# One fp32 transformer program on a single NeuronCore: norms and rotations moved beside dense tiles, token parts handled one by one

## What is computed

```python
def first_block(x, c, ...):            # 512 tokens
    h = _rms(x, norm1_w) * (1 + sc1) + sh1
    x = x + g1 * _hybrid_mixer(h, ...)     # SSD scan, dilated attention, pooling, gated and summed
    h = _rms(x, norm2_w) * (1 + sc2) + sh2
    x = x + g2 * (jnp.square(jax.nn.relu(h @ w_ff1)) @ w_ff2)
# in the mixer, for the scan's output y, in 2 groups of 512 columns:
    y = y * silu(z); y = y * lax.rsqrt(mean(y*y) + EPS); y_ssd = (y * ssd_norm_w) @ w_ssd_out
def second_block(x, c, ctx, c_ctx, ...):   # 4 layers over 512 latent + 256 context tokens
    for i in range(4):                 # mixers: window attention, latent attention, mLSTM, window attention
        h_l = rmsnorm(x_lat, g_pre) * (1.0 + sc_l) + sh_l
        h_c = rmsnorm(x_ctx, g_pre) * (1.0 + sc_c) + sh_c
        y_l, y_c = mixer(h_l, h_c, need_ctx=i < 3)
        x_lat = x_lat + gt_l * rmsnorm(y_l, g_post)
        if i < 3: x_ctx = x_ctx + gt_c * rmsnorm(y_c, g_post)
# latent attention (layer 1): q = rmsnorm(q_a) @ w_uq ; k, v = rmsnorm(kv_a) @ w_ukv ;
#   64 rotary columns of each query head and one shared rotary key are turned (RoPE)
# mLSTM (layer 2): two directions of decayed attention, summed, times sigmoid(o), rmsnorm by head, times silu(z)
```

## Time and profile before

| | us |
|---|---|
| median of 3 runs (lowest, highest) | 3195.63 (3194.22, 3197.38) |
| profiled execution: its own time | 3197.4 |
| profiled execution: span | 3195.6 |
| PE busy in the span | 2837.3 (89%) |
| DVE, ACT, POOL busy | 1682.6, 1216.8, 744.9 |
| mean granted TensorE clock | 0.947 of full |

### The profile page before, as it was taken

One profiled execution on the slowest core, in us unless ns is written; L12 is line 12 of the kernel. 1 busy time (PEld: TensorE's weight loads), 2 busy tenths in 40 slices (PEclk: granted clock), 3 DMA queues, 4 the chain that ended last, 5 costly groups with the idle time before them and its releaser, 6 DMA issues.

```text
span 3195.6 us, 39586 instructions
## 1 busy us (share of the span) xinstructions
PE 2837.3 (89%) x16088; PEld 2304.7 (72%) x16088; DVE 1682.6 (53%) x3080; ACT 1216.8 (38%) x2119; POOL 744.9 (23%) x160
## 2 busy tenths in 40 slices
PE   4976989989899999989898897899899988879896
PEld 2844877768686788769686675677589987658685
DVE  5875295162724999930387511254680246460483
ACT  3334224543123222242286333443442336342482
POOL 2410434304342444412100121100123210114101
PEclk7988999999899999999999998999999999899998
DMA  6402462202324555421101121101211331112101
GB/s 255 168 27 85 185 237 106 106 1 82 116 95 156 184 185 197 158 92 63 43 2 41 53 80 39 40 1 53 79 54 67 140 125 40 66 66 85 47 2 66
DMA packets 49621, 294.80 MB, mean 92 GB/s; under 512 B 4448, under 2 KB 5792, under 8 KB 19616
## 3 DMA queue, kind: packets, MB, share of 16 engines
q1 hardware_dynamic: 22464, 163.59, 14.2%
q10 hardware_dynamic: 26976, 128.68, 10.6%
HBM read 271.25 MB, written 21.00 MB: 91 GB/s over the span
## 4 chain that ended last, share of the span: by engine, by line
PE 61%; DVE 19%; ACT 4%; issue 3%; DMA 0%; ACTq 0%; DVEq 0%
PE psum L414 15%; PE psum L415 15%; PE psum L416 15%; DVE ada_temp L725 5%; PE psum L1636 2%; PE psum L873 2%; PE psum L1478 2%; PE psum L2783 2%; PE psum L1501 1%; PE psum L1657 1%; DVE pair_row L1686 1%; PE psum L1646 1%; DVE a_lo L882 1%; PE psum L1482 1%; DVE h L896 1%
## 5 line engine op out<-in xcount | busy, mean ns | idle before, releaser
L401 POOL TENSOR_TENSOR w_lo<-raw,w_hi 128x2048 fp32r<-128x2048 f32 x156 | 744.7, 4774 | 2408.7 <-ACT w_hi L409 2408.7
L414 PE MATMUL psum<-a_hi,w_hi 128*128 128x512 f32 (+3 forms) x1880 | 710.1, 378 | 105.5 <-DVE a_lo L882 66.5
L415 PE MATMUL psum<-a_lo,w_hi 128*128 128x512 f32 (+3 forms) x1880 | 699.3, 372 | 0.0
L416 PE MATMUL psum<-a_hi,w_lo 128*128 128x512 f32 (+3 forms) x1880 | 698.0, 371 | 0.0
L414 PEld LDWEIGHTS psum<-a_hi,w_hi 128*128 128x128 f32 (+1 forms) x1880 | 357.0, 190 | 193.8 <-issue 72.7
L725 DVE SCALAR_TENSOR_TENSOR ada_temp<-ada_ring,ada_rows 128x1024 f32<-128x1024 f32 x240 | 425.6, 1829 | 88.3 <-ACT ada_rows L685 54.6
L416 PEld LDWEIGHTS psum<-a_hi,w_lo 128*128 128x128 f32 (+1 forms) x1880 | 357.0, 190 | 63.1 <-issue 2.0
L415 PEld LDWEIGHTS psum<-a_lo,w_hi 128*128 128x128 f32 (+1 forms) x1880 | 357.6, 190 | 61.3 <-issue 3.2
L409 ACT ACTIVATE w_hi<-raw 128x2048 fp32r<-128x2048 f32 x156 | 298.0, 1911 | 246.6 <-DMA raw<-stream 98.2
L414 PE MATMUL psum<-w_hi,a_hi 128*128 128x256 f32 x800 | 229.6, 287 | 0.5 <-ACT c_gate_rows L2655 0.5
L415 PE MATMUL psum<-w_lo,a_hi 128*128 128x256 f32 x800 | 226.3, 283 | 0.0
(11 more groups left out here) (379 smaller groups left out, 4649.3 us busy)
## 6 DMA issues: line engine op xcount, KB each, us to landing
raw<-stream SPq DMA_DIRECT2D x156, 1024.0 KB, 4.8
ada_ring<-ada ACTq DMA_DIRECT2D x72, 1024.0 KB, 5.3
xres<-x_in ACTq DMA_DIRECT2D x4, 3072.0 KB, 9.5
x_in<-xres ACTq DMA_DIRECT2D x3, 3072.0 KB, 11.4
gates<-gate_part ACTq DMA_DIRECT2D x8, 768.0 KB, 4.4
c_rows_m<-rows_m ACTq DMA_DIRECT2D x2, 1536.0 KB, 7.9
c_og<-gates ACTq DMA_DIRECT2D x4, 768.0 KB, 4.2
c_z<-gates ACTq DMA_DIRECT2D x4, 768.0 KB, 6.4
```

The costliest lines, as they stand in the source:

```text
L401: pool.tensor_tensor(k.w_lo[:, r], k.raw[:, r], k.w_hi[:, r].bitcast(F32), ALU.subtract) \
L414: pe.matmul(out, lhs[0], rhs[0], start=start, stop=False)
L415: pe.matmul(out, lhs[0], rhs[1], start=False, stop=False)
L416: return pe.matmul(out, lhs[1], rhs[0], start=False, stop=stop)
```

## The change

1. `feature_major` puts out the LAT tiles of a pair of chunks, then their CTX tiles (before: LAT, CTX, LAT, CTX). `tile_place(t, n_parts)` gives chunk and part of tile t; all users of these tiles follow it. `pre_norm` says that CTX is waited for at tile 2, no more at tile 1.
2. `dense` gets `lead`: with `lead=2` the first two tiles are worked through together, product by product. Used in the first dense stage of all four layers (A0q, Bin, Cqk, A3q) and in ff1_0. In layer 3, whose q stage has no CTX tiles, the wait for CTX moves to the stage A3k.
3. `ssd_out`: both barriers go; DVE starts a group when its root is there, and PE goes on into the gates, waiting for chunk f of `y` only at the tile that reads it.
4. `layer_out` with two parts: `EarlySum` sums and roots LAT beside the last CTX tiles (behind tile 14 of the 16 tiles, 0 to 15); CTX's sum and root follow behind the barrier, and DVE starts on LAT as soon as the barrier is over. Its dense stage has 7 banks.
5. `mla_layer`: `LatentSteps` does norms, splits and the key's swap as a side of Bz, `QueryTurns` the query rotations as a side of Bk. The barriers behind Bz and Bq, and those of the steps, go; the one behind Bk stays. Bz, Bq and Bk have 6 banks.
6. Layer 2: no barrier between Cz and the attention. ACT loads head 0's gate at once, makes the decays of units 0 to 2, and only then waits for the stores. ACT's `scale` goes; DVE does that multiplication.

```diff
 def dense(... side=None, lead=1):
+                together = lead if lead > 1 and (i, s) == (0, 0) else 0
+                if together:
+                    pe.wait_ge(free.sem, free.at(together - ring))
+                    for j in range(len(slot_tiles[0][1])):
+                        if rhs_ready and (j, 0) in rhs_ready:
+                            pe.wait_ge(*rhs_ready[j, 0])
+                        for n, (cut, pairs) in enumerate(slot_tiles[:together]):
+                            last = products(pe, cut(bank(n)), *pairs[j], j == 0, j == len(pairs) - 1)
...
-    k.rhs_ready = split_at
+    k.rhs_ready = {(c, 2 * n): split_at[c, n] for c, n in split_at}
...
 def ssd_out(k, block, a, acc):
...
-    k.end_stage(block)
...
-    k.end_stage(block)
-    gated(k, block, a, y, [...], acc, B0, ada=...)
+    gated(k, block, a, y, [...], acc, B0 + 94208, rhs_ready=y_ready, ada=...)
...
+class EarlySum:
+    def on_tensor(self, pe, t):
+        if t == self.at:
+            pe.wait_ge(k.tile_free.sem, self.added)
+            pe.matmul(k.psum[:, 7, 0:t1 - t0], k.cst("ones"), self.total[:, t0:t1], ...)
+    def on_scalar(self, act, t):
+        if t == self.at:
+            act.wait_ge(self.summed.sem, self.summed.at(1))
+            root_rows(self.k, act, self.rstd, [self.part], D, (7,))
...
+class LatentSteps:
+    def on_scalar(self, act, t):
+        if t < 3:
+            act.activation(self.squares[:, t], self.raw[:, t, :], ACT.Square).then_inc(self.squared.sem, 1)
+        if t in (3, 5):
+            r = t // 2 - 1
+            act.wait_ge(self.summed.sem, self.summed.at(r + 1))
+            root_rows(k, act, self.rstd[:, r], [LAT, CTX], (256, 128)[r], (6, 7))
+    def on_tensor(self, pe, t):
+        if t in (1, 2, 4):
+            c = min(t - 1, 2)
+            pe.wait_ge(self.squared.sem, self.squared.at(c + 1))
+            if c == 2:
+                pe.wait_ge(self.rooted.sem, self.rooted.at(1))
+            for n, (t0, t1) in enumerate((LAT, CTX)):
+                last = pe.matmul(k.psum[:, 6 + n, 0:t1 - t0], k.cst("ones"), self.squares[:, c, t0:t1], ...)
+        if t == 7:
+            pe.wait_ge(self.rooted.sem, self.rooted.at(2))
+            pe.matmul(k.psum[:, 6, :], k.cst("swap"), self.raw[:, 3, 0:S], start=True, stop=True)
...
+class QueryTurns:
+    def on_tensor(self, pe, t):
+        n, rest = divmod(t, 5)
+        if rest == 0 and n < len(self.chunks):
+            if n >= 2:
+                pe.wait_ge(self.done.sem, self.done.at(n - 1))
+            pe.matmul(self.k.psum[:, 6 + n % 2, :], self.k.cst("swap"), self.chunks[n], start=True, stop=True)
...
 def decayed_attention(...):
-            dve.reciprocal(st[:, r, 2:4], st[:, r, 0:2]).then_inc(inverse.sem, 1)
-            dve.wait_ge(scaled.sem, scaled.at(n + 1))
-            dve.scalar_tensor_tensor(hsum[:, r], acc(n, 1)[:, 0:256], st[:, r, 3:4], forward[:, r], ALU.mult,
-                                     ALU.add).then_inc(taken.sem, 1)
+            ch(dve, dve.reciprocal(st[:, r, 2:4], st[:, r, 0:2]))
+            ch(dve, dve.tensor_scalar(hsum[:, r], acc(n, 0)[:, 0:256], st[:, r, 2:3], None, ALU.mult))
+            dve.scalar_tensor_tensor(hsum[:, r], acc(n, 1)[:, 0:256], st[:, r, 3:4], hsum[:, r], ALU.mult, ALU.add) \
```

More of the change, by code:

```diff
@@ L2160, in add_square @@
     def add_square(dve, i, t, ps):
-        t0, t1 = parts[t % n_parts]
+        t0, t1 = part(t)
         sq = square[:, t % 2, 0:t1 - t0]
@@ L2355, in mla_layer @@
           act_tile=lambda act, i, t, ps: (into(q, ACT.Copy, 0, -B_SCALE) if t < 16
-                                          else into(qr, ACT.Copy, -8, -B_SCALE))(act, i, t, ps))
+                                          else into(qr, ACT.Copy, -8, -B_SCALE))(act, i, t, ps),
+          barrier=False, n_banks=6)
     kv = [x[:, 2:3, :] for x in low]
@@ L2376, in take, with _ @@
         return act.activation(v[:, b, 512 * c:512 * c + 512], ps, ACT.Copy)
-    dense(k, block, ["Bk"], kv_tiles, act_tile=take)
-    rotate(k, block, [qr[:, c, 0:S] for c in range(4)], R0 + 73728)
+    @block.scalar
+    def _(act):
+        act.wait_ge(steps.normed.sem, key_turned)
+    turns = QueryTurns(k, [qr[:, c, 0:S] for c in range(4)], R0 + 92160)
+    dense(k, block, ["Bk"], kv_tiles, act_tile=take, n_banks=6, side=turns)
+    turns.over()
     b2 = (k.at("b2_hi", R0 + 24576, [P, KC, T2], F32R), k.at("b2_lo", A0, [P, KC, T2], F32R))
@@ L2631, in span @@
     def span(t):
-        n = S if t % 2 == 0 else SC
-        return n, (S if t % 2 else 0)
+        part = tile_place(t, 2)[1]
+        return (SC if part else S), (S if part else 0)
     def place(c):
         return 2 * (c % 4) + c // 4
-    dense(k, block, ["Cqk"], feature_major(a, KC, both), barrier=False,
+    dense(k, block, ["Cqk"], feature_major(a, KC, both), barrier=False, lead=2,
           act_tile=lambda act, i, t, ps: act.activation(pad[:, t % 8, 2:2 + span(t)[0]], ps[:, 0:span(t)[0]],
@@ L2847, in _ @@
                 decays(n + 1)
-            if 1 <= n <= N:
-                scale(n - 1)
+            if n == 1:
+                for place in range(3):
+                    act.wait_ge(saved[place].sem, 16 * len(range(place, 8, 3)))
+                load_z(0)
+                load_gate(1)
+                load_z(1)
             if n >= 2:
```

249 lines of the change are left out of this document (170 added, 79 removed).

## The result

The changed kernel takes **3101.9 us** (median of 4 runs, 3101.0 to 3107.4) beside 3196.5 us for the kernel before on the same chip: a ratio of 0.9707, with 0.9690 to 0.9723 as its interval. The forecast was 3097, in a range of 3085 to 3119. In another set, on another chip, the same program took 3102.6 us and the ratio was 0.9692 (0.9678 to 0.9706), so the ratio itself moves by some 0.15% from set to set.

A forecast was written before the change was run, and what follows sets the result against it. PE, busy 89% of the span, bounds the kernel; time is won in its pauses. Terms 18.3 + 21.2 + 12.0 + 25.0 + 9.0 + 7.5 + 7.0 = 100.0 us off 3197.4 give 3097.4, taken as 3097; range 3085 to 3119.

The forecast's parts named there:

- Two of my own signs of being wrong: PE waiting for ACT's root in Bz or for `y` in `gated`; a stage that the change leaves alone growing.
- `ssd_out`: Between norms' sums and gates: PE goes on without its 18.37 us stop; 18.3 us saved, lower bound 15.
- one rival: Moved DVE work beside dense tiles is held by POOL's splits, making the kernel slower: 3204 us, chance 0.01.
- Layer starts: First tile pairs of four layers: second LAT tile fits into the first's waits; 21.2 us with ff1_0, bounds 14 and 24.
- for ff1_0 [...] I estimate 0.5 of a possible 2: First feed-forward stage: two tiles together gain little because the start runs at half clock; 0.5 us saved.
- Layer ends: Three layer ends: LAT's early sum and root let DVE start 4.0 us earlier each; 12.0 us, bounds 6 and 13.
- 16.08 us follow to the next norm's first chunk, set by DVE's queue, and stay: Layer ends: the time from DVE's start to the next norm's first chunk stays 16.08 us.
- Behind Bz, Bq and Bk: Layer 1: pauses behind these stages go; 25.0 us behind Bz (bounds 20, 26), 9.0 behind Bq and Bk (4, 11).
- The rotations' 9.0: Query rotations moved into Bk: 6.6 us of pause and 2.4 of half clock at the attention's start saved.
- Side work in PE's way: Waits of `EarlySum`, `LatentSteps` and `QueryTurns` stop the dense tiles behind them: 3115 us, chance 0.10.
- The Trainium skill's 2.66 us for a table switch: Roots take 7.7 us, PE waits in Bz and at layer ends, the sum is 13 us smaller: 3110 us, chance 0.03.
- Layer 2: Pause before the attention shrinks, 7.5 us (bounds 4, 9.5); its units' stops at heads' roots shrink, 7.0 us (2, 10).

The follow-up runs named there:

- The idle matmuls: Changed kernel plus matmuls nobody reads in PE's pauses at layer starts and ends (3, 2 and 4), first feed-forward product one tile at a time: 3092.0 us.
- the doubled roots: Changed kernel with each of LatentSteps' two roots in stage Bz calculated twice: 3120.2 us, median of three runs.
- the other version: Changed kernel with fewer idle matmuls in PE's pauses (2, 1 and 3), first feed-forward product one tile at a time: 3093.0 us, ratio 0.9665.

## Why the prediction was right, and where it was not

The forecast was 4.9 us below the median, and the sum of 100.0 stands against 95.5 measured. It is right by its steps in most places, and partly because errors cancel. One slip helped too: the sum of 3097.4 less the 1.8 us to the median is 3095.6, and I wrote 3097. Two of my own signs of being wrong have to be answered: PE never waits for `y` in `gated`, nor for a root in Bz, but a stage that the change leaves alone, the third ff2, did grow, by 2.9 us.

- **`ssd_out`.** 18.3 forecast, 18.0 measured. The near agreement is luck. PE goes on at full clock, which gave 1.7 us that I had not counted, and the norms' own sums ran longer, partly at half clock (0.64 over 268 to 272), which lost 2.1 (15.0 us from the first sum to the gates, where 12.9 were to stay); two variants without that loss have 20.6 at this place. The stop's absence also costs time in the third ff2 stage, 2.8 us by putting the barriers back, which I had not counted either. POOL held one of the moved casts, `y_hi`, for 4.72 us instead of 0.43, as one rival had it, and PE did not wait for it.
- **Layer starts.** 5.4 us each and 4.5 for layer 3: measured 5.35, 5.3, 5.25 and 4.0 to 4.7. The stop went from 3.86 to 2.95 us, forecast 3.2. The step that failed is the last clause, "for ff1_0 [...] I estimate 0.5 of a possible 2": the sign is wrong, the pair costs 1.8 us by itself and up to 4.6 with where the clock falls. I looked at what PE gains and not at who waits for the first tile. ACT and DVE do, and a modulation chain stands behind it.
- **Layer ends.** 12.0 forecast, 7.6 measured. DVE's start came 4.9 us nearer to the last tile, where 5.3 were forecast (4.0, and the 1.3 by which that tile was to end later). What failed is "16.08 us follow to the next norm's first chunk, set by DVE's queue, and stay". They became 17.3 to 18.2 us, 4.9 more in the three ends together. The chain had passed to ACT and PE: sums at half clock, with DVE idle for 1.3 to 2.1 us. The idle matmuls show it. 2.8 us were lost in layer 0's dense stage, where 1.3 were forecast: its first tile ran at half clock for some microseconds in this profile, and in other variants that stage took 68.1 us instead of 69.8.
- **Behind Bz, Bq and Bk.** 25.0 and 9.0 forecast. Measured are 23.3, 9.3 of pause behind Bk, and 4.5 in the attention. The rotations' 9.0 was made of 6.6 us and 2.4 of clock. I had PE as the bound of Bk with the swaps in it, for some 3 us; they cost nothing or 2.0 us, by the clock. The clock's part was 1.7 us in the first step with the rotations put behind Bk, and 2.8 in the profile of the kernel before; the other 1.7 of its 174.5 us is the second step, which also came out long in nine of twelve traces with the change, so that part is not the change's.
- **Side work in PE's way** did not come true. PE waits for none of the side steps in Bz. But the roots were covered with 0.1 to 0.2 us to spare and not 0.5 to 0.9; the doubled roots show how near this rival was. The Trainium skill's 2.66 us for a table switch (ScalarE: Activation LUTs, What ACT_TABLE_LOAD costs) is contradicted here a second time. The doubled root added four switches in two roots and 9.7 us of stops, which is what loads of 1.28 us give.
- **Layer 2.** 7.5 forecast for the pause, 8.2 measured, 7.3 by undoing it. 7.0 forecast for the units, 10.6 measured, 8.5 by undoing `scale`: the term was mis-sized, by leaving the clock out. The three stops gave 5.9 us, as expected. Behind two of them the kernel before ran at a lower clock: the next unit took 8.9 and 7.6 us at 0.67 and 0.78 of the full clock, where it takes 6.5 at 1.00, and that gave 3.5. The last 1.2 are at the start, where the first scores ran at 0.60 of the clock behind the long pause and now run at 1.00.

## What to carry to other kernels

When a wait is taken out of a chain, read the next engine's share of that chain under the new timing, its clock included: a queue that "stays" was set by one engine only as long as the others had slack. Before two tiles are computed together, ask who needs the first of them. And a stop of PE inside dense work cost one and a half times its length here, while a pause of 7.8 us in front of layer 2's attention cost 7.3; filling pauses in front of work that someone waits for is worth it, filling them in front of work that waits for others is not. Last, where the low clock falls moves a section by 1.7 to 2.3 us from one trace to the next, so two single traces can't show a smaller effect without the clock beside it.

## What the runs showed of the hardware that was not expected

**A DVE operation can be held for as long as a POOL split lasts, and a few tenths of a microsecond decide it.** In the third ff1 stage DVE has four modulation products in a row. In the kernel before, the fourth started at 1197.04, and POOL's split at 1197.13; in the changed kernel, POOL's split came first. DVE's and POOL's timelines, before:

```profile
1197.04 1.22 DVE L725 SCALAR_TENSOR_TENSOR ada_temp<-ada_ring,ada_rows 128x1024 f32<-128x1024 f32 x1
...
1198.19 0.70 DVE L2051 TENSOR_TENSOR psum<-psum,r 128x512 f32<-128x512 f32 x1
...
1197.13 5.61 POOL L401 TENSOR_TENSOR w_lo<-raw,w_hi 128x2048 fp32r<-128x2048 f32 x1 [3.98 <-ACT w_hi L409]
```

and in the changed kernel:

```profile
1184.69 5.62 DVE L748 SCALAR_TENSOR_TENSOR ada_temp<-ada_ring,ada_rows 128x1024 f32<-128x1024 f32 x1
...
1183.92 5.30 POOL L401 TENSOR_TENSOR w_lo<-raw,w_hi 128x2048 fp32r<-128x2048 f32 x1 [3.46 <-ACT w_hi L409]
```

The held one took 5.62 us instead of 1.22. ACT's next slot copy and the split behind it came 2.9 us later for it, and the ff2 stage that follows is 2.9 us longer. All fourteen traces fit. Counted from the stage's start, the split comes at 8.2 us in each. In the kernel before and with the barriers of `ssd_out` back, the fourth product starts at 8.10 and 8.16 us, ahead of it, and the ff2 stage takes 44.0 and 44.05 us. In the twelve others it starts at 8.41 to 8.98 us, is held for 5.6 us, and the stage takes 46.4 to 47.8. Operations with an operand in PSUM were not held: the square on `psum` beside the split took 0.70 us. A single input in SBUF did not keep an operation free, however: the cast `y_hi<-z` beside a split took 4.72 us, where its like takes 0.43. The Trainium skill (SBUF — State Buffer, SBUF: two separate sides) states the rule: a GpSimd operation and a DVE operation that has two SBUF inputs, or runs in a 2-port perf mode (it then also uses the ports that it shares with GpSimd), exclude each other for the whole instruction, and the one that starts first goes on; for the two inputs this holds only where GpSimd reads SBUF, as the split does. The trace agrees, with 5.62 us for two inputs; that the cast ran in such a mode is not shown.

**Idle matmuls that nobody reads keep the clock at its higher level.** At the end of layer 2 in the changed kernel it stands at about 0.5 (1.2 GHz) behind pauses of 1.96 and 3.17 us. At the end of layer 0, with the two pauses of this kind filled but for 0.35 us in the first, it stays at 1.00 (2.4 GHz), and with 1.11 and 1.04 us left open in the other version too. It did fall behind the pause of 3.7 us that was left as it was.
